# Two routings of a two-block kernel: activation tables loaded ahead, picks turned beside the running sum, and identity products on TensorE between the steps

## What is computed

```python
def expert_choice_moe(h, w_router, w_gate, w_up, w_down):
    cap = max(1, CAPACITY_FACTOR * S // N_EXPERTS)              # 32 rows for each of 16 experts
    logits = jnp.einsum('bsd,de->bse', h, w_router)
    aff = jax.nn.softmax(logits, axis=-1)
    gate, idx = lax.top_k(aff.transpose(0, 2, 1), cap)
    xin = jax.vmap(lambda hb, ib: hb[ib])(h, idx)
    hid = jax.nn.silu(einsum('becd,edf->becf', xin, w_gate)) * einsum('becd,edf->becf', xin, w_up)
    y = einsum('becf,efd->becd', hid, w_down) * gate[..., None]
```

## Time and profile before

| | |
|---|---|
| median of 3 runs | 1281.4 us (1279.88 to 1282.64) |
| the profiled execution | 1280.97 us, span of its instructions 1279.2 us |
| TensorE (PE) busy | 1096.4 us, 86% |
| VectorE (DVE) busy | 402.8 us, 31% |
| ScalarE (ACT) busy | 202.4 us, 16% |
| GpSimd (POOL) busy | 123.1 us, 10% |
| chain that ended last | PE 63%, DMA 30%, DVE 4%, ACT 2% |
| read from HBM | 375.09 MB, 294 GB/s over the span |
| mean granted TensorE clock | 0.942 of full |

### The profile page before, as it was taken

One profiled execution on the slowest core, in us unless ns is written; L12 is line 12 of the kernel. 1 busy time (PEld: TensorE's weight loads), 2 busy tenths in 40 slices (PEclk: granted clock), 3 DMA queues, 4 the chain that ended last, 5 costly groups with the idle time before them and its releaser, 6 DMA issues.

```text
span 1279.2 us, 19614 instructions
## 1 busy us (share of the span) xinstructions
PE 1096.4 (86%) x8744; PEld 618.4 (48%) x8744; DVE 402.8 (31%) x820; ACT 202.4 (16%) x420; POOL 123.1 (10%) x148
## 2 busy tenths in 40 slices
PE   7999997987667666766699999999999979999796
PEld 6744545442222222222254546888878655455332
DVE  5256844011001000100026866552166351111103
ACT  3221422000000000000000012211132032222111
POOL 0010000010001893000003630000000000000000
PEclk9999997999878879878899999999999989999999
DMA  9423848999999999999972564311245768999992
GB/s 330 156 79 122 333 189 333 428 427 428 427 427 427 428 427 427 427 429 426 424 283 71 185 199 160 130 69 68 79 164 226 292 233 361 426 426 425 424 423 115
DMA packets 58565, 379.01 MB, mean 296 GB/s; under 512 B 5743, under 2 KB 7279, under 8 KB 36719
## 3 DMA queue, kind: packets, MB, share of 16 engines
q1 hardware_dynamic: 56992, 370.69, 71.3%
q10 hardware_dynamic: 1486, 7.03, 1.7%
HBM read 375.09 MB, written 1.05 MB: 294 GB/s over the span
## 4 chain that ended last, share of the span: by engine, by line
PE 63%; DMA 30%; DVE 4%; ACT 2%; issue 1%; SPq 0%; DVEq 0%; ACTq 0%
DMA arena<-in_w_expert_up 22%; PE psum L489 12%; PE psum L492 9%; PE psum L2881 5%; PE psum L1394 3%; PE psum L856 3%; PE psum L2290 3%; DMA arena<-in_expert_w_in 3%; DMA arena<-in_w_expert_gate 3%; PE psum L2525 3%; PE psum L2905 3%; PE psum L2871 2%; PE psum L1424 2%; PE psum L2386 2%; PE psum L1103 2%; DMA arena<-in_w_expert_down 2%
## 5 line engine op out<-in xcount | busy, mean ns | idle before, releaser
L1394 PE MATMUL psum<-arena 128*32 128x256 f32 x2048 | 150.2, 443 | 92.6 <-DMA arena<-in_w_expert_up 56.1
L489 PE MATMUL psum<-arena 128*128 128x512 f32 x352 | 157.6, 598 | 3.2 <-ACT arena L526 1.6
L1394 PEld LDWEIGHTS psum<-arena 128*32 128x32 f32 x2048 | 70.3, 123 | 173.6 <-DMA arena<-in_w_expert_up 72.3
L1424 PE MATMUL psum<-arena 128*32 128x512 f32 x512 | 127.7, 653 | 16.0 <-DMA arena<-in_w_expert_down 11.2
L492 PE MATMUL psum<-arena 128*128 128x256 f32 x544 | 123.0, 382 | 1.0 <-ACT arena L1838 1.0
L492 PEld LDWEIGHTS psum<-arena 128*128 128x128 f32 x544 | 101.6, 189 | 17.0 <-issue 2.2
L489 PEld LDWEIGHTS psum<-arena 128*128 128x128 f32 x352 | 64.8, 190 | 81.4 <-issue 81.1
L2881 PE MATMUL psum<-arena 128*32 (+2 forms) x608 | 73.7, 615 | 8.1 <-DMA arena<-in_expert_w_in 6.5
L1424 PEld LDWEIGHTS psum<-arena 128*32 128x32 f32 x512 | 32.5, 119 | 99.0 <-issue 73.2
L1455 DVE TENSOR_TENSOR arena<-arena,psum 128x256 f32<-128x256 f32 x16 | 6.8, 422 | 221.8 <-ACT arena L1438 221.8
L1562 POOL TENSOR_TENSOR arena<-arena 128x16 f32<-128x16 f32 (+6 forms) x64 | 43.6, 682 | 151.6 <-DMA arena<-in_ssm_bc 146.7
(11 more groups left out here) (480 smaller groups left out, 1203.8 us busy)
## 6 DMA issues: line engine op xcount, KB each, us to landing
arena<-in_w_expert_gate SPq DMA_DIRECT2D x32, 2048.0 KB, 25.2
arena<-in_w_expert_up SPq DMA_DIRECT2D x32, 2048.0 KB, 26.2
arena<-in_w_expert_down SPq DMA_DIRECT2D x31, 2048.0 KB, 24.2
arena<-in_expert_w_in SPq DMA_DIRECT2D x28, 2048.0 KB, 19.9
arena<-in_w_in SPq DMA_DIRECT2D x21, 2048.0 KB, 8.7
arena<-in_expert_w_down SPq DMA_DIRECT2D x32, 1024.0 KB, 17.2
arena<-in_w_out SPq DMA_DIRECT2D x4, 2048.0 KB, 7.7
arena<-in_expert_w_in SPq DMA_DIRECT2D x8, 1024.0 KB, 10.5
```

Source lines behind the costliest of these rows:

```text
L489: mm = pe.matmul(o, lhs[:, k, sub * P:(sub + 1) * P], w[:, k, :], start=(k == 0), stop=(k == kt - 1))
L1394: mm = pe.matmul(ps[32 * c:32 * c + 32], xin[:, e, k], w[:, j, 256 * n:256 * n + 256], start=(k == 0), stop=(k == KD - 1))
L1424: mm = pe.matmul(y_ps[at:at + 32, 512 * n:512 * n + 512], hid_T4[:, j, half], w[:, j, 512 * n:512 * n + 512], start=(half == 0 and j == 0) ...
```

## The change

- In `out_and_route` the fourth group of turns gets a bank of its own (bank 1, free once the projection has been added) and goes ahead of all router products.
- The third group of turned rows is copied by ScalarE instead of VectorE, under a semaphore of its own, `n2_T_third`.
- ScalarE executes an unread Sqrt of one column before the squares, and an unread Exp of one column right after the square root.
- `highest(0)` comes before the setting of `ones_row`.
- The first round reads the turned affinities in PSUM; the copy to `work` is gone. The rounds count up `r_round`.
- The picks are turned as soon as they are there, and the running sum after it; the product of the two is made after both turns, on 128x32 instead of 16x256.
- `keep_busy(pe, b, n)` multiplies the identity by `n` columns of itself into a bank that nobody reads. There are seven in block 1's routing (five of 384 columns, two of 256) and six in block 2's (512, 512, 384, 512, 128, 256), each between two steps.

```diff
     "rw_D_turned": ("n1_spread", 1), "e1_y1": ("n1_ones", 1), "rw_DT_odd": ("e1_y1", 4), "e1_y": ("n1_root_ready", 1),
-    "b2_turned": ("n1_turned", 4), "pu_product": ("p1_product", 6), "ssm_b_turned": ("p2_product", 4),
+    "b2_turned": ("n1_turned", 4), "r_round": ("p1_product", 6), "pu_product": ("r_round", 5),
+    "n2_T_third": ("p2_product", 4), "ssm_b_turned": ("n2_T_third", 1),
...
+        def keep_busy(pe, b, n):
+            pe.matmul(b[:, 0:n], ident, along(ident, n // P, 1), start=True, stop=True)
+
...
-            turned = [bank(5), bank(6), bank(7), bank(5)]
+            turned = [bank(5), bank(6), bank(7), bank(1)]
...
                 turn(1, 0)
+                turn(1, 1)
                 route(0, range(4))
-                turn(1, 1)
                 route(0, range(4, KD))
                 route(1, range(4))
                 route(1, range(4, KD))
 
+                keep_busy(pe, bank(5), 384)
                 pe.wait_ge(*count("r_aff", 1))
                 for t in range(NT):
                     mm = pe.transpose(bank(1)[0:E1, t * P:(t + 1) * P], aff[:, t], ident)
                 mm.then_inc(inc("r_aff_turned"), 1)
-                pe.wait_ge(*count("r_slots", 1))
-                for t in range(NT):
-                    mm = pe.transpose(bank(6)[:, t * E1:(t + 1) * E1], place[0:E1, t * P:(t + 1) * P], ident[0:E1, 0:E1])
-                mm.then_inc(inc("r_slots_turned"), 1)
+                keep_busy(pe, bank(5), 384)
+                for n in range(CAP // 8 - 1):
+                    pe.wait_ge(*count("r_round", n + 1))
+                    keep_busy(pe, bank(5), 384)
+                for a, (sem, n), src in ((0, ("r_round", CAP // 8 + 1), picked), (NT * E1, ("r_slots", 1), place)):
+                    pe.wait_ge(*count(sem, n))
+                    for t in range(NT):
+                        mm = pe.transpose(bank(6)[:, a + t * E1:a + (t + 1) * E1], src[0:E1, t * P:(t + 1) * P], ident[0:E1, 0:E1])
+                    if a:
+                        mm.then_inc(inc("r_slots_turned"), 1)
+                    keep_busy(pe, bank(5), 256)
...
+                act.activation(unread, ident[:, 0:1], ACT.Sqrt)
                 for n in range(4):
                     act.wait_ge(*count("o1_out0", n + 1))
                     square(n, n // 2, slice(512 * (n % 2), 512 * (n % 2) + 512))
+                act.wait_ge(*count("n2_turned", 3))
+                act.activation(x2_T[:, 0:4, P:2 * P], turned[2].rearrange("p (k s) -> p k s", k=4), ACT.Copy)\
+                   .then_inc(inc("n2_T_third"), 1)
                 act.wait_ge(*count("n2_ms", 1))
                 act.activation(sd, ms, ACT.Sqrt).then_inc(inc("n2_sd"), 1)
+                act.activation(unread, ident[:, 0:1], ACT.Exp)
                 act.wait_ge(*count("n2_rs", 1))
...
-                w = work[0:E1]
-                step(dve.tensor_copy(w, bank(1)[0:E1, 0:SEQ]))
-                for _ in range(CAP // 8):
-                    step(dve.max(best[0:E1], w))
-                    step(dve.match_replace(w, best[0:E1], w, -1.0))
-                step(dve.tensor_scalar(picked[0:E1], w, -0.5, None, ALU.is_lt))
-                step(dve.tensor_tensor_scan(place[0:E1], ones_row[0:E1], picked[0:E1], 0.0, ALU.mult, ALU.add))
-                dve.tensor_tensor(place[0:E1], place[0:E1], picked[0:E1], ALU.mult).then_inc(inc("r_slots"), 1)
+                w, still = work[0:E1], bank(1)[0:E1, 0:SEQ]
+                for n in range(CAP // 8):
+                    step(dve.max(best[0:E1], still))
+                    ins = dve.match_replace(w, best[0:E1], still, -1.0)
+                    ins.then_inc(inc("r_round"), 1)
+                    dve.wait_ge(*count("r_round", n + 1))
+                    still = w
+                dve.tensor_scalar(picked[0:E1], w, -0.5, None, ALU.is_lt).then_inc(inc("r_round"), 1)
+                dve.wait_ge(*count("r_round", CAP // 8 + 1))
+                dve.tensor_tensor_scan(place[0:E1], ones_row[0:E1], picked[0:E1], 0.0, ALU.mult, ALU.add)\
+                   .then_inc(inc("r_slots"), 1)
                 dve.wait_ge(*count("r_slots_turned", 1))
-                step(dve.tensor_copy(slot_of, bank(6)[:, 0:NT * E1]))
+                step(dve.tensor_copy(slot_of, bank(6)[:, NT * E1:2 * NT * E1]))
+                step(dve.tensor_tensor(slot_of, slot_of, bank(6)[:, 0:NT * E1], ALU.mult))
...
             def tensor(pe):
+                keep_busy(pe, bank(6), 512)
+                pe.wait_ge(*count("r2_gmax", 1))
+                keep_busy(pe, bank(6), 512)
+                pe.wait_ge(*count("r2_emax", 1))
+                keep_busy(pe, bank(6), 384)
                 pe.wait_ge(*count("r2_chosen", 1))
                 for t in range(NT):
                     mm = pe.transpose(bank(5)[0:E2, t * P:(t + 1) * P], er[:, t], ident)
                 mm.then_inc(inc("r2_er_turned"), 1)
+                keep_busy(pe, bank(6), 512)
                 pe.wait_ge(*count("r2_ranks", 1))
                 pe.matmul(bank(4)[0:1, 0:E2], rank[0:E2, SEQ - 1:SEQ], ident[0:E2, 0:E2], start=True, stop=True)\
                   .then_inc(inc("r2_counts"), 1)
+                keep_busy(pe, bank(6), 128)
                 pe.wait_ge(*count("r2_local", 1))
                 for t in range(NT):
                     mm = pe.transpose(bank(7)[:, t * E2:(t + 1) * E2], er_T[0:E2, t * P:(t + 1) * P], ident[0:E2, 0:E2])
                 mm.then_inc(inc("r2_turned_back"), 1)
+                keep_busy(pe, bank(6), 256)
```

More of the change, by code:

```diff
@@ L112 @@
     "rw_scaled": ("hg_ms", 1), "rw_T": ("hg_rows", 1), "rw_products_out": ("hg_out", 2),
-    "rw_inv": ("o1_out0", 4), "rw_xv_out": ("n2_ms", 1), "rw_state": ("n2_rows", 2), "rw_x": ("n2_T", 4),
+    "rw_inv": ("o1_out0", 4), "rw_xv_out": ("n2_ms", 1), "rw_state": ("n2_rows", 2), "rw_x": ("n2_T", 3),
     "rw_y": ("r_max", 2), "rw_gn_ms": ("r_aff", 1), "rw_y_rows": ("r_slots", 1), "rw_out": ("r_chosen", 2),
@@ L1136, in turn @@
                     pe.wait_ge(*count("o1_out0", 2 * t + half + 1))
-                    if (t, half) == (1, 1):
-                        pe.wait_ge(*count("n2_T", 1))
                     for j in range(4):
@@ L1144, in route @@
                 def route(t, ks):
-                    pe.wait_ge(*count("n2_T", 2 * t + ks[-1] // 4 + 1))
+                    if (t, ks[0]) == (1, 0):
+                        pe.wait_ge(*count("n2_T_third", 1))
+                    else:
+                        pe.wait_ge(*count("n2_T", min(2 * t + ks[-1] // 4 + 1, 3)))
                     for k in ks:
@@ L1276, in vector @@
                 dve.tensor_scalar(ms, ms, RMS_EPS, None, ALU.add).then_inc(inc("n2_ms"), 1)
-                copy_turned(1, 0)
                 copy_turned(1, 1)
@@ L1280, in vector @@
                 dve.reciprocal(rs, sd).then_inc(inc("n2_rs"), 1)
+                highest(0)
                 dve.memset(ones_row, 1.0)
-                highest(0)
                 highest(1)
```

2 lines of the change are left out of this document (1 added, 1 removed).

## The result

| | before | after |
|---|---|---|
| median, same chip | 1280.8 us (4 runs, 1279.9 to 1282.6) | 1271.7 us (4 runs, 1270.0 to 1272.5) |
| the profiled execution | 1280.97 us, span 1279.2 us | 1271.99 us, span 1270.2 us |
| mean granted TensorE clock | 0.942 | 0.959 |

The ratio is 0.9928, interval 0.9914 to 0.9941: 9.1 us faster, where 0.9 was forecast.

The account below looks back on a forecast made before the run. The prediction took the DMA weight stream, restarted after each routing's gather, as the bound. Its terms, -0.25 - 0.45 - 0.22 + 0.03 = -0.9 us, with the clock worth 0, gave 1280.5 us; range 1276.5 to 1283.0.

Parts of the forecast that it names:

- The path and the stream: Both routings: each us by which a gather ends earlier moves the DMA weight stream and the end by one us.
- The sum of -0.9 us for tables, PSUM and picks: Block 1's routing: table loads ahead -0.25, first round from PSUM -0.45, picks turned beside the sum -0.22, products in the way +0.03.
- TensorE's new order: Block 1, before the logits: fourth turn ahead of the router products leaves the logits' end at 194.86 us; gain 0.
- MAX8 out of PSUM: Block 1's first round: MAX8 reading 16x256 from PSUM takes no surcharge, with 0.1 us as the upper end.
- The 0.03 for products in the way: Both routings: identity products delay TensorE's next steps at two tight places by 0.03 us, between 0 and 0.6.
- The step that failed: Both routings: identity products too light to hold TensorE's clock; half clock when each gather starts, so worth 0.
- rival 1: TensorE's clock holds at full through both routings: 5.3 us more gained, 1275.2 us; chance 0.12.
- the fall at 195.2 us: Block 1's routing: clock fell after only 0.3 us idle behind thin 16-column products, taken as evidence that gaps alone don't decide.
- my doubt: Both routings: the skill's rule that avoiding long idle gaps keeps the clock up was doubted; how little TensorE multiplies counts too.
- every saving on in full: Both routings: savings reach the end undiminished while under DMA's idle time, about 6 us in block 1, over 3 in block 2.

Follow-up runs that it names:

- the version with eight more and the two of 512 columns: Changed kernel plus eight 16-column identity products behind block 1's router products and two 512-column ones in block 2's recurrence branch: 1272.86 us, ratio 0.9949.

## Why the prediction was wrong

**The path and the stream.** Right. The gathers moved the stream of weights: the offset between the profiles is -1.8 us at the first expert product and still -1.6 at 650 us, at the end of the experts' stage that DMA bounds. The sum of -0.9 us for tables, PSUM and picks was about right. From the first turn to the gather the gain is 1.13 us (1.18 without products). Of that 0.29 lies before the end of the logits, where the prediction gave TensorE's new order 0; the other 0.84 is what it summed up. The ratio without products, 0.9993, agrees with 0.9 us but does not show it. MAX8 out of PSUM has no surcharge. The 0.03 for products in the way was a little low: the turn of the slots starts 0.19 us after the running sum ended, behind a 256-column product, where such a hand-over took 0.06 before.

**The step that failed** is the one on the clock: "256 columns cost 0.40, 384 about 0.60 and 512 about 0.80 us", and from it "one such product per round fills 0.60 of 0.96 us at half clock, 63%". The earlier trace rows give 0.40 us for one *record* of 256 columns, and a float32 product is two records. The earlier trace rows say so: L1184 is called for 8 x 2 products there, and stands as x32 (a turn is one record). A 384-column product took 1.17 us at 195.95, partly at full clock, not 0.60; so at half clock it fills the round. The "24 products" and "32 products" of 16 columns in the prediction are records too, 12 and 16 products.

The version with half the columns multiplies 192 columns twice, the 384 that I had reckoned with. It behaves as I forecast: half clock from 195.8 to 206 us, into the gather, and gathers of 5.46 and 5.95 us. The full product was back at full clock after 3.4 us. So the mechanism was right for the amount that I took, and the amount was half of the real one.

The comparison by busy share with the earlier trace rows was no help either. From 196.5 to 199.8 us the changed kernel was busy for 2.94 of 3.3 us, 89%, and the version with half the columns for 6.33 of 7.3 us, 87%, yet only the first got its clock back soon. Without that step rival 1 had no row against it but the fall at 195.2 us, and it is close to what happened: its 5.3 us are 4.6 as measured (2.4 between the 16-column version and the changed kernel in turns to expert, 20.41 against 17.99, and 2.2 in block 2, 26.08 against 23.88). In block 1 the clock did not hold but came back in time, and the gathers at full clock took 4.13 and 3.81 us, not 3.7 and 3.6.

The Trainium skill could have caught it. FP8 and Floating Point Precision, "TensorE Precision Notes", has a true float32 product make four passes through the array. Four passes of 384 columns at 1.2 GHz are 1.28 us, an estimate from that page, beside the 1.17 measured with a part at full clock. On the rule of the Trainium skill that the prediction cites from TensorE: Matmul & The Clock Gate, the runs agree with my doubt: thirteen thin products (16 columns) did not keep the clock up, although TensorE never stood idle between them for more than 1.10 us.

**What the prediction had no term for** is the 3.2 us in the recurrence branch. I moved "every saving on in full", but asked of unchanged code only whether it hides a saving, never whether it depends on how many instructions stand ahead of it. The row of 2.84 us "<-issue" was in the trace before. Nor did I ask for DMA queues other than the weights'.

**The sum as it came out**: 1 us from tables and picks, 4.6 from the clock in both routings, 3.2 from instructions that come in time; 8.8 of 9.1 us. That it closes so well is partly luck. In the two profiles, 8.98 us apart, block 1's first turn comes 1.5 us later in the changed kernel (190.71 against 189.18 us), and between the burst and block 2's router products 1.7 us are won (4.2 us ahead at 876.96, 5.95 at 1021.43). The first is not the change: with block 1's products alone the turns start at 189.16 us. The second is the size of the half clock that only the kernel before has there (953.0 to 956.4 us, lie in it), and the kernel before once more does not have it. Why such short falls come and go stays open.

## What to carry to other kernels

Filling a clocked-down wait works only with products that are heavy enough, and their weight must be taken from a row that covers whole products, with its count of records checked against the loop; too thin ones (16 columns) cost 0.38 us each at half clock and hold nothing. An idle time under "issue" in the middle of a dense burst is worth a look at the instruction queue: if a large transfer runs across it that isn't needed soon, start that one later. Here one wait gave 6.8 us in the kernel before, though nothing clear of the scatter in the changed one. And a change that adds or removes instructions can move or shorten such a stop far behind it (some 680 us here), so an ablation has to keep their number, as the 16-column version does.

## What the runs showed of the hardware

- A 16 KB instruction packet came 8.8 us after the one before it when a 2 MB weight transfer ran, 5.8 us after it when the transfer started later, and TensorE went on 1.4 to 1.6 us after the packet's end in twelve profiles. With 16 more records ahead it stopped 16 records earlier.
- An identity product of 512 columns at full clock is two records, 1.02 to 1.13 us (block 2's routing of the changed kernel); eight float32 products of 16 columns took 3.01 us, nearly all at half clock, 0.38 us each, and each has two 128x128 weight loads.
- In block 1's routing the clock came back after 3.4 us in all six profiles with the full products and nothing more there, after 10.2 with half the columns, after 13.6 with 16 columns, and after 13.6 or 13.7 in the seven profiles with none. In block 2 the full products kept it from falling at all in most profiles (both of the changed kernel), but with block 2's products alone it fell for 3.4 us (from 1038.5 us), and so it did in the version with eight more and the two of 512 columns (from 1034.1); both times it was back before the gather. Why some executions differ was not tried.
- A table load of ScalarE beside TensorE's logits cost the path nothing, and its 1.28 us were the same in either place.
